# Moving two normalisation sums behind the second projection, and the lambda and mask work ahead of an attention stage

## The reference

```python
def rmsnorm(x, g):
    xf = x.astype(jnp.float32)
    y = xf * lax.rsqrt(jnp.mean(xf * xf, axis=-1, keepdims=True) + EPS)
    return (y * g.astype(jnp.float32)).astype(x.dtype)
...
hn = rmsnorm(h, a_norm_g[i])                            # layer A
qkv = (hn @ a_w_qkv[i]).reshape(B, T, 3, SB_HEADS, SB_HEAD_DIM)
...
kvn = rmsnorm(h, kv_norm_g); kv = kvn @ kv_w            # layer B
lam = jnp.exp(jnp.sum(lp[0] * lp[1])) - jnp.exp(jnp.sum(lp[2] * lp[3])) + lam_init
q1 = apply_partial_rope(rmsnorm(qq[..., 0, :], b_q_norm_g[j, 0]), cos, sin)
w = probs(q1b, k1f) - lam * probs(q2b, k2f)             # causal softmaxes
```

## Time and profile before

| | |
|---|---|
| median of 3 runs (2780.4 to 2786.22) | 2782.85 us |
| the profiled execution, its own time | 2780.4 us |
| its span | 2778.6 us |
| PE busy | 2597.3 us (93%) |
| DVE busy | 1135.4 us (41%) |
| ACT busy | 1032.5 us (37%) |
| POOL busy | 840.6 us (30%) |
| mean granted TensorE clock | 0.985 of 2.4 GHz |

### The profile page before, as it was taken

How to read it: one execution, slowest core, us unless ns; L and a number is a source line. 1 busy time by engine, 2 the same in 40 slices (tenths; PEclk the granted TensorE clock), 3 DMA queues, 4 the chain that set the end, 5 groups by cost and what they waited for, 6 DMA issues and landing times.

```text
span 2778.6 us, 41957 instructions
## 1 busy us (share of the span) xinstructions
PE 2597.3 (93%) x16786; PEld 2124.4 (76%) x16786; DVE 1135.4 (41%) x2012; ACT 1032.5 (37%) x2128; POOL 840.6 (30%) x532
## 2 busy tenths in 40 slices
PE   8999899999978888888999989999999999999999
PEld 6877788888855555555888869999999887778877
DVE  7754666232242111111456653232247776512212
ACT  5444454442222111112455554322334555432231
POOL 1002565213311222100311106645641110465563
PEclk9999999999989999999999999999999999999999
DMA  4330111433349999997211112323322111233331
GB/s 146 84 78 23 31 39 32 114 84 97 98 181 390 426 427 426 426 424 322 69 46 54 46 39 76 94 83 90 99 86 68 47 46 32 60 91 95 102 94 65
DMA packets 311731, 370.43 MB, mean 133 GB/s; under 512 B 10208, under 2 KB 283744, under 8 KB 286960
## 3 DMA queue, kind: packets, MB, share of 16 engines
q1 hardware_dynamic: 310384, 363.52, 37.6%
q0 software_dynamic: 1152, 4.19, 0.4%
HBM read 363.49 MB, written 4.19 MB: 132 GB/s over the span
## 4 chain that ended last, share of the span: by engine, by line
PE 66%; DMA 12%; DVE 9%; ACT 5%; POOL 4%; issue 3%; ACTq 0%; SPq 0%; DVEq 0%; POOLq 0%
DMA early<-in_w_up_e 11%; PE bank L2300 5%; PE bank L1823 5%; PE bank L2301 4%; PE bank L2302 4%; PE bank L2793 4%; PE bank L2794 4%; PE bank L2795 4%; PE bank L442 4%; PE bank L443 4%; PE bank L444 4%; POOL split L2275 2%; DVE early L683 2%; PE bank L3055 1%; PE bank L1060 1%
## 5 line engine op out<-in xcount | busy, mean ns | idle before, releaser
L2275 POOL TENSOR_TENSOR split<-keep,split 128x1024 fp32r<-128x1024 f32 x143 | 354.1, 2481 | 451.1 <-ACT split L2249 451.1
L2300 PE MATMUL bank<-x_hi,split 128*128 128x264 f32 (+1 forms) x1280 | 397.6, 311 | 12.3 <-POOL split L2275 9.5
L2301 PE MATMUL bank<-x_lo,split 128*128 128x264 f32 (+1 forms) x1280 | 390.2, 305 | 0.0
L2302 PE MATMUL bank<-x_hi,split 128*128 128x264 f32 (+1 forms) x1280 | 389.8, 305 | 0.0
L2249 ACT ACTIVATE split<-keep 128x1024 fp32r<-128x1024 f32 x192 | 200.3, 1050 | 222.7 <-PE bank L2795 208.0
L1823 PE MATMUL bank<-early 128*64 128x256 f32 x2048 | 236.5, 384 | 44.1 <-DMA early<-in_w_up_e 36.3
L2300 PEld LDWEIGHTS bank<-x_hi,split 128*128 128x128 f32 x1280 | 241.0, 188 | 34.3 <-issue 19.7
L1823 PEld LDWEIGHTS bank<-early 128*64 128x64 f32 x2048 | 166.9, 138 | 125.1 <-issue 78.7
L2301 PEld LDWEIGHTS bank<-x_lo,split 128*128 128x128 f32 x1280 | 241.2, 188 | 9.9 <-issue 0.2
L2302 PEld LDWEIGHTS bank<-x_hi,split 128*128 128x128 f32 x1280 | 240.1, 188 | 10.2
L2831 DVE TENSOR_TENSOR mlp<-mlp,bank 128x264 f32<-128x264 f32 (+1 forms) x96 | 49.5, 516 | 326.5 <-ACT mlp L2810 326.5
(11 more groups left out here) (476 smaller groups left out, 6062.5 us busy)
## 6 DMA issues: line engine op xcount, KB each, us to landing
early<-in_w_gate_e SPq DMA_DIRECT2D x64, 1024.0 KB, 11.1
early<-in_w_up_e SPq DMA_DIRECT2D x64, 1024.0 KB, 12.0
early<-in_w_down_e SPq DMA_DIRECT2D x64, 1024.0 KB, 11.8
early<-in_w_in SPq DMA_DIRECT2D x68, 512.0 KB, 3.6
keep<-in_mlp_w_in SPq DMA_DIRECT2D x64, 512.0 KB, 3.9
keep<-in_mlp_w_out SPq DMA_DIRECT2D x64, 512.0 KB, 4.0
keep<-in_a_w_qkv SPq DMA_DIRECT2D x24, 512.0 KB, 3.7
early<-in_w_ssd_out SPq DMA_DIRECT2D x16, 512.0 KB, 4.0
```

Of the source, the lines that this page charges most:

```text
L2275: e.tensor_tensor(lo, x, whole(hi), ALU.subtract).then_inc(*u.free(sig_, "lo", n))
L2300: e.matmul(o, hi[:, k, :], xh, start=k == 0, stop=False, skip_group_check=True)
L2301: e.matmul(o, hi[:, k, :], xl, start=False, stop=False, skip_group_check=True)
L2302: m = e.matmul(o, lo[:, k, :], xh, start=False, stop=k == 7, skip_group_check=True)
```

## The change

Three edits.

1. `NA1.sums_pe` (layer A) moves from behind the first projection to behind the second.
2. `NB.sums_pe` (layer B) moves in the same way; `turn_pe(e, 0, 1)` still follows it.
3. The lambda and mask work becomes a stage of its own (`normb_act`, `normb_dve`) between the MLP and layer B. PE's wait for "mask" moves from the first score to the first line of `attb_pe`.

```diff
@@ atta_pe
                         linear_pe(e, PA, n, ("qk", p, j), HALVES2, normed(NA1) if p == j == 0 else None)
-                        if p == j == 0:
+                        if p == 0 and j == 1:
                             NA1.sums_pe(e, HALVES2, TILESA)
@@
-        def lambda_act(e):
+        def normb_act(e):
             e.wait_ge(*LM.dve.to("lam"))
             e.activation(sm[:, 0:2], sm[:, 0:2], ACT.Exp).then_inc(*LM.act.up("lam"))
             for y, x in ((IDENT2, C["ident"]), (NEG2, C["amask"][:, 128:256])):
                 e.activation(y, x, ACT.Copy).then_inc(*LM.act.up("mask"))
-        def lambda_dve(e):
+        def normb_dve(e):
             lam4 = C["lam"].rearrange("p (a b n) -> p a b n", a=2, b=2)
             e.wait_ge(*Z0.dve.to("x", 3, 7))
...
+        program.append((None, normb_act, normb_dve, None, None))
...
-        ATTB.insert(4, ("lambda", 0))
@@ attb_pe
         def attb_pe(e):
+            e.wait_ge(*LM.act.to("mask"))
...
                         linear_pe(e, PD, n, ("qkb", p, j), HALVES2, normed(NB) if p == j == 0 else None)
-                        if p == j == 0:
+                        if p == 0 and j == 1:
                             NB.sums_pe(e, HALVES2, TILES2)
...
-                    if i == 0:
-                        e.wait_ge(*LM.act.to("mask"))
@@ attb_act, attb_dve
-                if what == "lambda":
-                    lambda_act(e)
...
-                if what == "lambda":
-                    lambda_dve(e)
```

## The result

Six runs of the changed kernel took 2802.19 to 2805.78 us, with a median of 2804.27; six of the kernel before took 2780.4 to 2788.65, with a median of 2784.53. The ratio is 1.0069, with a 95% interval of 1.0058 to 1.0080: 19 us slower (16 to 22). All 15 runs recorded with this result took 2800.75 to 2807.43 us.

A forecast was written before the change was run, and what follows sets the result against it. It took PE, busy 93% of the span, as the bound. Edit 1's 4.2, edit 3's 5.4, edit 2's 3.4 and the clock's 5.2 made 18.2 us on 2780.4: 2798.6, plus 2.45 to the median, forecast 2801; range 2790 to 2809.

The forecast's parts named there:

- loss of 4.2 us: Layer A: PE's third projection would start at 1371.4 instead of 1367.2, held until the first projection's banks are read.
- 1.5 us of slack: Layer A: weight piece 3 split until 1375.8, wanted by the fourth projection at 1377.3, so its later load costs nothing.
- 5.88 us of the sum: Pace of one projection on PE, taken from layer B's timeline and used to place later starts.
- upper bound: Before layer B: DVE's lambda product held until POOL's addition ends, masks at 2077.4; the lower bound, not held, gave 2076.1.
- gains' row: Layer B's norm: DVE's multiplication by the gains took 2.35 us during a POOL addition, 1.22 in another of the same form.
- three stops at 1.7 us each: PE stops of about 5.5, 3.1 and 3.2 us, each followed by 3.9 us of dense work at half clock.
- 4.1 and 3.3 us: Edit 1's loss and edit 2's exposed chain as added into the range's lower case, 2792, without a clock loss.
- The clock stays at 1.00: Rival: the waits come but PE's clock does not fall; 13.0 us more, 2796; chance 0.13.
- Only the mask wait counts: Rival: third projections aren't held, only PE's wait before layer B costs; 7.1 us more, 2790; chance 0.06.
- nothing: Rival: the shift is taken up by PE's waits in the attention stages; 2783; chance 0.04.
- Faster: Rival: stretches the change doesn't touch regain full clock, up to 37 us back, 2759 at the far end; chance 0.02.

The follow-up runs named there:

- second execution of the changed kernel: The kernel with all three edits, nothing altered, run and profiled again; median 2804.41 us, ratio 1.0077 to the kernel before.
- kernel with other banks: Edit 1 alone against the kernel before, with layer A's third projection in two banks of the other ring; ratio 1.0008.
- filled kernel: Changed kernel plus spare unused matmuls (23, 24 and 40) in PE's three long stops; 2797.99 us, ratio 1.0055 to the kernel before.
- kernel with the late wait: Edit 3 alone against the kernel before, but PE's wait for the mask left at the first score; ratio 1.0004.
- kernel with the masks first: Edit 3 alone against the kernel before, with ACT's two mask copies ahead of its wait for the lambda sums; ratio 1.0012.
- edits 1 and 2 alone: Two kernels, each with only that one edit made to the kernel before; ratio 1.0027 for edit 1, 1.0021 for edit 2.

## Why the prediction was right, point by point

The forecast was 2801 us from a base of 2782.85, 18.2 us more; measured were 2804.27 and 19 us more, inside 2790 to 2809. Of the 3.3 us between the two times, 1.7 are the base: the kernel before had a median of 2784.53 beside the changed one.

- **Edit 1, waits.** Forecast a wait of about 1.2 us for DVE's split and 3.1 us for the banks; in the profile 1.36 and 3.00. The loss of 4.2 us stands: the second execution of the changed kernel lost 5.8 us in layer A, of which 1.5 are one half-clock stretch. The kernel with other banks shows the banks to be what PE waited for.
- **Edit 1, the moved DMA queue.** Forecast no cost, with 1.5 us of slack. In the changed kernel no wait for POOL's split appears there, and none in the filled one, where the third projection ran at full clock and took the 5.88 us of the sum. With the third projection free to start 3 us earlier it appears at once, at 1.44 us: near 3.0 less the slack of 1.5.
- **Edit 3.** Forecast a lambda product held to 1.4 us and a loss of 5.4; in the profile 1.39 and a wait of 5.42, with the first projection 5.3 us later behind the MLP's last matmul than before. The choice of the upper bound, from the gains' row, was right. That the work itself is free was forecast and is shown by the kernel with the late wait. That the masks sat behind the lambda chain on ACT was in the code; that this order was worth 2.1 us is shown by the kernel with the masks first.
- **Edit 2.** Forecast a stop of 3.2 us before the head sums; in the profile 3.22.
- **The clock.** Forecast three stops at 1.7 us each, 5.2 us. For these three the traces of the changed kernel show 5.1 and 5.7 us, and the filled kernel's time is 6.4 us lower. The size of the single stops was less well met: behind the masks they lost 2.2 and 1.6 us, behind the head sums' wait 1.4 and 2.6, behind the banks' wait 1.6 and 1.5. That the sum came out at 5.2 owes something to chance. The forecast left out a fourth stretch behind the 1.36 us wait, which cost 1.6 us in the first profiled execution and nothing in the second. This, and not a wait, makes up the difference between 18.2 and the 19.6 us of the first execution.
- **The range.** Its lower end is added up from 4.1 and 3.3 us where the forecast has 4.2 and 3.4; it would be 0.2 us higher, which changes nothing.
- **Rivals.** "The clock stays at 1.00" is out by the filled kernel. "Only the mask wait counts" is out by edits 1 and 2 alone, "nothing" by all three. Nothing behind gave the shift back: the edits' own waits and stretches come to 19.6 us, where 19 (16 to 22) were measured. "Faster", by half-clock stretches elsewhere going away, did not come: the part between the two places was no shorter in any of the nine profiled executions with a change (699.9 to 705.8 us, against 698.6).

No version beat the kernel before. The best ones here only take the edits' costs away again, and their intervals hold 1.

## What to carry to other kernels

A step that looks like an interruption between two pieces of PE work (here the sums) can be the head of a chain that the next piece covers. Before moving it back, find who frees the buffers of the piece after next, and count what would still cover the chain. A wait belongs where its result is used; here the work could be moved early for nothing, the wait could not. And a stop on a busy PE can cost more than its length: here 13 us of waits cost 19.

## What the runs showed of the hardware that was not expected

- Filling three stops with matmuls that compute nothing made the kernel 6.4 us faster (2797.99 against 2804.41 us): the stops kept their lengths, and PEclk stayed at 1.00 behind them.
- A PE wait of only 1.33 to 1.36 us was followed by a stretch at half clock in three of five profiled executions: the changed kernel (0.53 from 1360.6 to 1363.8), edit 1 alone, and the filled kernel (0.50 from 1358.6 to 1361.8). In the kernel with other banks it was not (1.00 from 1360 to 1380), nor in the second execution of the changed kernel (1.00 from 1359.4 to 1365.2), so the same code goes both ways. Why is open. The unfilled waits of 3 us and more that the edits made were all followed by half clock in the profiles.
- A DVE product of 128x128 elements took 1.38 to 1.42 us beside a POOL addition, and 0.28 us without it.
